# Gate sums inside the Fourier unit's products, constant products in TensorE's waits, and the cross-attention memory loaded early

## The reference

```python
g = (p[..., OFF_G:OFF_BR].astype(jnp.float32).reshape(b, l, N_GATE_KINDS, N_H).transpose(2, 0, 3, 1)
     + b_gates.astype(jnp.float32)[:, None, :, None])
...
h_f, s_f = mlstm_scan(q, k, v, g[0], jax.nn.log_sigmoid(g[1]), init[0])
...
u = p[..., OFF_F:OFF_QK].astype(jnp.float32).reshape(b, l, N_FG, FG)
fu = jnp.fft.fft2(u, axes=(1, 3), norm='ortho').real.astype(p.dtype).reshape(b, l, D_F)
...
y_m = (jax.nn.sigmoid(p[..., OFF_O:OFF_G]) * hm) @ w_mlstm
...
logf = jax.nn.log_sigmoid(f_logit.astype(jnp.float32) + fox_bf[l].astype(jnp.float32))
...
x = x + cross_attention(rmsnorm_2(x, norm_xa_g[l]), rmsnorm_2(mem, norm_mem_g[l]), ...)
...
g_logits = (hf @ wg).astype(jnp.float32) + bg.astype(jnp.float32)
e_logits = ((hf @ we).astype(jnp.float32) + be.astype(jnp.float32)).reshape(-1, N_GROUPS, EXPERTS_PER_GROUP)
```

## Time and profile before

| | |
|---|---|
| median of 3 runs | 1780.99 us (1780.74, 1780.99, 1786.05) |
| the profiled execution | 1787.18 us, span 1785.4 us |
| PE busy | 1686.0 us, 94% |
| DVE busy | 726.2 us, 41% |
| ACT busy | 400.8 us, 22% |
| mean granted TensorE clock | 0.977 of full speed |
| DMA | 374.35 MB, mean 210 GB/s over the span |

### The profile page before, as it was taken

The page is one execution under the profiler, slowest core; times in us unless marked ns, Lnnn a source line. Parts: engine busy times, 40 slices in busy tenths (PEclk is TensorE's granted clock), DMA queues, the critical chain, the costliest instruction groups (busy, mean ns, idle before and its releaser), DMA issues. The chain is left out here.

```text
span 1785.4 us, 21495 instructions
## 1 busy us (share of the span) xinstructions
PE 1686.0 (94%) x8607; PEld 951.5 (53%) x8607; DVE 726.2 (41%) x1337; ACT 400.8 (22%) x737; POOL 22.1 (1%) x29
## 2 busy tenths in 40 slices
PE   6998999998999999999999989999999999877987
PEld 3576456657886534443444333444478664454543
DVE  4644513656546011111111115974762424351425
ACT  5112112442214101010101031015641023210112
POOL 0000000000000000000000000000000000000001
PEclk9998999999999999999999999999999999988999
DMA  9421157101133999999999970411112231269974
GB/s 364 137 86 47 71 193 278 48 32 67 67 141 118 398 425 423 421 418 426 424 419 419 426 293 0 142 47 48 47 63 80 94 135 77 94 263 381 325 271 177
DMA packets 88934, 374.35 MB, mean 210 GB/s; under 512 B 9796, under 2 KB 10132, under 8 KB 73748
## 3 DMA queue, kind: packets, MB, share of 16 engines
q1 hardware_dynamic: 82084, 350.14, 50.0%
q10 hardware_dynamic: 3712, 12.06, 1.8%
q0 software_dynamic: 3056, 11.01, 1.7%
HBM read 466.51 MB, written 10.49 MB: 267 GB/s over the span
## 5 line engine op out<-in xcount | busy, mean ns | idle before, releaser
L2236 PE MATMUL bank<-H,weight_slots 128*128 128x512 f32 (+1 forms) x704 | 286.3, 565 | 4.1 <-ACT H L808 2.9
L2236 PEld LDWEIGHTS bank<-H,weight_slots 128*128 128x128 f32 x704 | 135.8, 195 | 149.2 <-issue 143.8
L2652 PE MATMUL bank<-weight_slots,SM 128*64 128x512 f32 x640 | 143.9, 595 | 9.4 <-DMA weight_slots<-in_w_up_e 9.4
L2337 PE MATMUL bank<-R,weight_slots 128*128 128x256 f32 x560 | 123.9, 380 | 0.0
L2680 PE MATMUL bank<-weight_slots,SM 128*64 128x512 f32 x384 | 114.6, 609 | 3.6 <-DMA weight_slots<-in_w_down_e 3.6
L2337 PEld LDWEIGHTS bank<-R,weight_slots 128*128 128x128 f32 x560 | 106.1, 190 | 15.7 <-issue 1.5
L2236 PE MATMUL bank<-R 128*128 128x128 f32 (+2 forms) x784 | 104.5, 286 | 9.5 <-DVE R L2088 6.2
L3028 PE MATMUL bank<-weight_slots,SM 128*32 128x256 f32 x1536 | 91.0, 390 | 21.3 <-DMA weight_slots<-in_expert_w_gate 11.5
L2236 PEld LDWEIGHTS bank<-R 128*128 128x128 f32 x784 | 94.4, 195 | 13.4 <-DVE R L2085 6.3
L2652 PEld LDWEIGHTS bank<-weight_slots,SM 128*64 128x64 f32 x640 | 45.4, 137 | 104.2 <-issue 84.1
L1762 DVE TENSOR_TENSOR R<-SM,bank 128x512 f32<-128x512 f32 x16 | 11.0, 687 | 217.7 <-PE bank L2652 217.7
(11 more groups left out here) (513 smaller groups left out, 2101.6 us busy)
## 6 DMA issues: line engine op xcount, KB each, us to landing
weight_slots<-in_expert_w_gate SPq DMA_DIRECT2D x51, 1024.0 KB
weight_slots<-in_expert_w_up SPq DMA_DIRECT2D x51, 1024.0 KB
R<-in_expert_w_down SPq DMA_DIRECT2D x51, 1024.0 KB
weight_slots<-in_w_up_e SPq DMA_DIRECT2D x24, 2048.0 KB, 17.3
weight_slots<-in_w_down_e SPq DMA_DIRECT2D x24, 2048.0 KB, 23.7
weight_slots<-in_w_in SPq DMA_DIRECT2D x18, 2048.0 KB, 9.5
weight_slots<-in_w_gate_e SPq DMA_DIRECT2D x16, 2048.0 KB, 17.0
weight_slots<-in_w_ada SPq DMA_DIRECT2D x12, 2048.0 KB, 10.7
```

What stands on the lines that cost most here:

```text
L2236: ins = nc.tensor.matmul(dst, lhsT, rhs, start=(i == 0), stop=(i == len(pairs) - 1))
L2337: ins = nc.tensor.matmul(bank_half(name, i, half)[:, TC * tile:TC * (tile + 1)], lhs[:, kk, m:m + 128], rhs[:, kk, :], start=(begins and k ...
L2652: ins = nc.tensor.matmul(b[64 * half:64 * half + 64, :], xs[:, 4 * rows + k, 64 * e:64 * e + 64], w[k][:, 512 * half:512 * half + 512], st ...
```

## The change

In unit `u`, the gate sums (now without bias products) stand behind P1 and the 12 transposes into rows behind P5; DVE and ACT do the gate arithmetic between the unit's additions and copies; all four folds stand behind the unit's last addition. The wait for the rows' copies before the q products is gone. The biases of gates, forget logits and router are broadcast to all partitions by the loads and added by DVE where it copied before. `keep_busy` multiplies constants (128 x 128 by 128 x 512) in four places: 2 before the k products, 3 before the last expert pair's down products, 6 before the ranking, 6 before `pick_rows`.

The memory is loaded by ACT in two DMAs behind unit `w_fourier`, into `H`'s context columns. It is transposed at its old place into banks 2, 3, 6 and 7, and copied by ACT. Its squares (ACT, behind the copy of P1) are summed with 32-column weights behind P5 of unit `w_mlstm`, and the four partial sums are folded behind P7; DVE scales the memory behind the unit's last addition. P1 of the unit waits only for heads 0 and 1, P2 for the rest.

```diff
+        m_rows = H[:, :, T:T + TC]
+        memT = R4[:, :].rearrange("p (k t) -> p k t", k=KD)
+        mem_sq = SM[:, 0:2048].rearrange("p (k t) -> p k t", k=KD)
+        MEM_BANKS = (2, 3, 6, 7)
...
-                sp.dma_start(rowb[0:1, 0:16], A["b_gates"].rearrange("a g h -> a (g h)")).then_inc(sem("rowb_in"), 16)
+                sp.dma_start(rowb[:, 0:16], A["b_gates"].rearrange("a g h -> a (g h)").broadcast_to([P, 16])).then_inc(sem("rowb_in"), 16)
...
+            u_copies("P1", "11")
             act.wait_ge(sem("gate_v"), 1)
             act.activation(absf, gts[:, :, :, 1, :], ACT.Abs).then_inc(sem("gate_s"), 1)
...
+            u_copies("P6", "12")
             act.wait_ge(*reached("rows_mm", 1))
-            act.activation(ig_r[:, 0:T], PS[1][0:36, :], ACT.Copy).then_inc(sem("rows_s"), 1)
+            act.activation(ig_r[:, 0:T], PS[2][0:36, :], ACT.Copy).then_inc(sem("rows_s"), 1)
+            u_copies("P7", "22")
+            u_copies("P4", "21")
...
             quarter_copies("w_fourier")
+            act.wait_ge(sem("thin_mm"), 1)
+            for t in range(2):
+                act.dma_start(m_rows[:, 4 * t:4 * t + 4, :], A["mem_2"][0, P * t:P * (t + 1), :].rearrange("p (q n) -> p q n", n=TC)).then_inc(sem("mem_in"), 16)
...
-            act.wait_ge(sem("S_mm"), 16)
-            act.dma_start(m_tok, A["mem_2"].rearrange("b (t p) d -> p (b t) d", p=P)).then_inc(sem("mem_in"), 16)
-            rms_squares(act, "nm", memT, sqc, TC, lambda k: act.wait_ge(sem("mT_ev"), k // 2 + 1))
-            rms_root(act, "nm", PS[5][:, 0:TC], std[:, T:T + TC])
-            quarter_copies("w_mlstm")
+            for j in range(4):
+                act.wait_ge(*reached("mT_mm", j + 1))
+                act.activation(memT[:, 2 * j:2 * j + 2, :], PS[MEM_BANKS[j]][:, :].rearrange("p (k t) -> p k t", k=2), ACT.Copy).then_inc(sem("mT_ev"), 1)
+            block_copies("w_mlstm", "P1", "11")
+            act.wait_ge(sem("attn_v"), 23 * NH)
+            for k in range(KD):
+                act.wait_ge(sem("mT_ev"), k // 2 + 1)
+                act.activation(mem_sq[:, k, :], memT[:, k, :], ACT.Square).then_inc(sem("rms_sq"), 1)
+            block_copies("w_mlstm", "P6", "12")
...
-            fold_u(2)
-            fold_u(3)
...
-            nc.vector.tensor_copy(gts, PS[0][:, 0:96].rearrange("p (t e c h) -> p t e c h", t=TA, e=2, c=2)).then_inc(sem("gate_v"), 1)
+            nc.vector.tensor_tensor(SM[:, 1024:1120].rearrange("p (t n) -> p t n", t=TA), PS[0][:, 0:96].rearrange("p (t n) -> p t n", t=TA),
+                                    rowb[:, 0:16].unsqueeze(1).broadcast_to([P, TA, 16]), ALU.add).then_inc(sem("gate_v"), 1)
...
+            for g in (2, 3, 0, 1):
+                fold_u(g)
+            dve.wait_ge(*reached("u_fold", 12))
             nc.vector.memset(cum_r, 0.0).then_inc(sem("rows_v"), 1)
...
-                rms_scale(dve, "nm", lambda k: memT[:, k, :], lambda k: H[:, k, T:T + TC], TC, std[:, T:T + TC], rstd2[:, T:T + TC], lambda k: v("mem", k))
...
-            plain_sums("w_mlstm", s2_mlstm, beside_mlstm, beside_last=lambda: weight_sums("brB0", s1, s2))
+            plain_sums("w_mlstm", s2_mlstm, beside_mlstm, beside_last=gate_weights)
+            rms_scale(dve, "nm", lambda k: memT[:, k, :], lambda k: H[:, k, T:T + TC], TC, std[:, T:T + TC], rstd2[:, T:T + TC], lambda k: v("mem", k))
...
+            def keep_busy(bank, times):
+
+                for i in range(times):
+                    nc.tensor.matmul(bank[:, :], ones, const[:, 0:512], start=True, stop=True)
...
-            wait_weights(pe, "k")
             for j in range(8):
                 b = take(j % 4, "conv_k", 3 * (j + 1) if j < 4 else 12 + 9 * (j - 3))
+                if j == 0:
+                    keep_busy(b, 2)
+                    wait_weights(pe, "k")
...
-                    first = [] if bias is None else [(ones[0:1, :], bias)]
-                    ins = product(dst[:, n * t:n * (t + 1)], first + [(parts[:, 128 * t:128 * (t + 1)], fold[:, 0:n])])
+                    ins = product(dst[:, n * t:n * (t + 1)], [(parts[:, 128 * t:128 * (t + 1)], fold[:, 0:n])])
...
-                   "P4": [(sem("quarter_ev"), ev + 5 + half) for half in range(2)], "P3": [(sem("quarter_add"), add + 2)] * 2})
-            thin_sum(take(0, "gate_v", 1), thin_gates, TA, 16, 2, rowb[0:1, 0:16]).then_inc(sem("gate_mm"), 1)
+                   "P4": [(sem("quarter_ev"), ev + 5 + half) for half in range(2)], "P3": [(sem("quarter_add"), add + 2)] * 2},
+                  behind={"P1": gates_summed, "P5": gates_turned})
...
-            pe.wait_ge(sem("rows_v"), 4)
             w = weights("q", KD)
...
-            rms_sum(pe, "nm", take(5, "rms_std", NORMS["nm"] + 1), sqc, TC)
-            pe.wait_ge(sem("attn_v"), 23 * 4)
-            seven_plain("w_mlstm", "mlstm", mlstm_in, mlstm_sums, s1_mlstm, s2_mlstm)
+            def memory_squares():
+                part = take(6, "rms_part", WIDE["nm"])
+                for k in range(KD):
+                    g = k % 4
+                    pe.wait_ge(sem("rms_sq"), KD * NORMS["nm"] + k + 1)
+                    nc.tensor.matmul(part[32 * g:32 * g + 32, 0:TC], ones[:, 0:32], mem_sq[:, k, :], start=(k < 4), stop=(k >= 4),
+                                     tile_position=(0, 32 * g)).then_inc(sem("rms_sum"), 1)
...
+            seven_plain("w_mlstm", "mlstm", mlstm_in, mlstm_sums, s1_mlstm, s2_mlstm, {"P1": (sem("attn_v"), 23 * 2), "P2": (sem("attn_v"), 23 * NH)},
+                        {"P5": memory_squares, "P7": memory_norm})
...
                 pe.wait_ge(sem("hidT_ev"), pair * 2 + 2)
+                if pair is last:
+                    keep_busy(PS[0], 3)
...
-            nc.tensor.matmul(b[:, 80:100], ones[0:1, :], rowb[0:1, 24:44], start=True, stop=True)
             thin_sum(b, thin, TT, 20, 5).then_inc(sem("rl_mm"), 1)
 
+            b = take(2, "token_slots", 2)
+            keep_busy(b, 6)
             pe.wait_ge(*reached("chosen", 1))
...
+            keep_busy(PS[0], 6)
             for name, value in (("xtok_v", 2 * TT), ("x_sq", 2 * TT), ("thin_ev", 5), ("g_v", 2), ("token_slots", 2)):
```

More of the change, by code:

```diff
@@ L64 @@
 KEY_BANKS = (0, 1, 4, 5)
-WIDE = {name: i + 1 for i, name in enumerate(["n1", "n2", "nf", "n3", "n4"])}
+WIDE = {name: i + 1 for i, name in enumerate(["n1", "nm", "n2", "nf", "n3", "n4"])}
 def key_done(j):
@@ L496, in build @@
         fourier_sums = [two(R6[:, 512 * i:512 * (i + 1)]) for i in range(4)]
-        mlstm_sums = [two(R4[:, 512 * i:512 * (i + 1)]) for i in range(4)]
+        mlstm_sums = [two(R2[:, 512 * i:512 * (i + 1)]) for i in range(4)]
         conv_sums = [two(c0_flat[:, 0:512]), two(c0_flat[:, 512:1024]), conv_in["12"], two(R2[:, 0:512])]
@@ L832, in _, with u_copies @@
             u_quarters = quarters(u_plain)
-            for which, quarter in (("P1", "11"), ("P6", "12"), ("P7", "22"), ("P4", "21")):
+            def u_copies(which, quarter):
                 for half in range(2):
@@ L908, in _ @@
                         gate_a(2 * h + 1)
-            act.wait_ge(sem("S_mm"), 16)
-            act.dma_start(m_tok, A["mem_2"].rearrange("b (t p) d -> p (b t) d", p=P)).then_inc(sem("mem_in"), 16)
-            rms_squares(act, "nm", memT, sqc, TC, lambda k: act.wait_ge(sem("mT_ev"), k // 2 + 1))
-            rms_root(act, "nm", PS[5][:, 0:TC], std[:, T:T + TC])
-            quarter_copies("w_mlstm")
+            for j in range(4):
[7 more added lines that the diff above has]
+            block_copies("w_mlstm", "P6", "12")
+            act.wait_ge(sem("rms_sum"), KD * NORMS["nm"] + KD)
+            act.activation(mem_parts, PS[6][:, 0:TC], ACT.Copy).then_inc(sem("rms_part"), 1)
+            block_copies("w_mlstm", "P7", "22")
+            act.wait_ge(sem("rms_fold"), WIDE["nm"])
+            act.activation(std[:, T:T + TC], PS[7][:, 0:TC], ACT.Sqrt, bias=small[:, 40:41], scale=1.0 / D).then_inc(sem("rms_std"), 1)
+            block_copies("w_mlstm", "P4", "21")
             def quarter_gates(name):
@@ L2342, in seven, with seven_plain @@
                         behind[which]()
-            def seven_plain(name, of, src, t, s1, s2):
+            def seven_plain(name, of, src, t, s1, s2, ready=None, behind=None):
                 ev, add = QUARTER_EV[name], QUARTER_ADD[name]
@@ L2348, in seven_plain @@
                       {"P6": [(sem("quarter_ev"), ev + 1 + half) for half in range(2)], "P7": [(sem("quarter_ev"), ev + 3 + half) for half in range(2)],
-                       "P4": [(sem("quarter_ev"), ev + 5 + half) for half in range(2)], "P3": [(sem("quarter_add"), add + 3 + half) for half in range(2)]})
+                       "P4": [(sem("quarter_ev"), ev + 5 + half) for half in range(2)], "P3": [(sem("quarter_add"), add + 3 + half) for half in range(2)]}, ready, behind)
             def seven_gates(name, of, src, t, s1, s2):
@@ L2392, in _, with gates_summed, gates_turned @@
             pe.wait_ge(sem("wsmall_in"), 80)
-            pe.wait_ge(sem("rowb_in"), 64)
```

(11 more changed lines are left out.)

92 lines of the change are left out of this document (43 added, 49 removed).

## The result

The changed kernel took 1756.79 us in the median of four runs (1755.57 to 1758.51), beside 1783.52 us for the kernel before in four runs. The ratio is 0.9839, with a 95% interval of 0.9814 to 0.9864: 28.7 us less, 24.3 to 33.2. (Every "less than before" in this document is worked out from such a ratio; the two medians themselves are 26.7 us apart.) The forecast was 27.9 us less than before, 1753 us, with a range of 1747 to 1763. The time is 3.8 us above 1753, and 2.5 us of that is the kernel before, whose median was 1780.99 us when the forecast was made. One of the eight runs of `gates_alone` in experiment 2, 2099.3 us at a granted clock of 0.80, was in a slow state and is left out of that kernel's ratio.

What follows compares the result with a forecast made beforehand. The prediction took PE's own chain, busy 94% of the span, to set the end. Its terms, 11.3 + 10.4 + 1.4 + 2.1 + 2.0 + 0.7 = 27.9 us, off the 1781.0 us median gave 1753 us, range 1747 to 1763.

Steps and rivals of the forecast that it cites:

- Fourier input, gates: From unit `u`'s end to the end of the q products, 42.4 us become 31.1: 11.3 us less.
- merge: Last head's end to P1 of `w_mlstm`, 14.4 us, with norm moved into the unit: 10.4 us less, bounds 8 to 11.
- before k: Constants in PE's 2.86 us wait before k bring the clock back sooner: 1.4 us less, bounds -0.6 to 1.9.
- forget logits: 8 of 16 small entries go, and perhaps the low-clock spell from 1163 us: 2.1 us less, bounds 1.3 to 3.0.
- last pair: Constants in the 3.64 us wait for a down weight warm the down products: 2.0 us less, bounds -1.3 to 2.6.
- router: Constants in the 6.43 us wait for `chosen` let ranking run warm: 0.7 us less, bounds -3.4 to 1.5.
- The reserve of DVE: Behind `u`, scans start at about 160.2 us; row chain ready about 170, wanted 183.4; kw products have 16 us in hand.
- the load stream keeps its time: Rival: first MoE's loads don't come earlier with PE, only 5 us remain, 1776 us; chance 0.04.
- Low clock in the units: Rival: inserted small products or transposes lower the clock inside the two units, 1.7 to 6.8 us, about 1757; chance 0.13.
- Late engines: Rival: DVE or ACT late in a unit brings the removed wait back, 4 to 10 us, about 1761; chance 0.08.
- Constants decide nothing: Rival: the clock follows other things and `keep_busy` gives nothing or outlasts its waits, 1757 to 1762 us; chance 0.05.
- Slower: Rival: inserts in `u` keep the clock at 1.2 GHz to the end of the q products, 1805 us; chance 0.02.

Runs made afterwards that it cites:

- gates_alone: Kernel before with only the Fourier input and gate part of the change, biases included: 1775.22 us, ratio 0.9948.
- experiment 2: The change's three parts (gates, memory, constants) each put alone into the kernel before, and the whole: 1775.22, 1773.77, 1780.24 and 1756.36 us.
- experiments 1: Kernel before profiled again without any edit: 1783.64 us beside 1784.83 us, ratio 0.9995.
- memory_alone: Kernel before with only the memory part (early load, transposes behind the last head, norm inside unit `w_mlstm`): 1773.77 us, ratio 0.9939.
- experiment 5: Changed kernel with four 128 x 128 transposes in place of each product of constants: 1759.70 us, ratio 0.9861.
- experiment 3: Changed kernel with 14 or 28 memsets delaying DVE's row chain behind unit `u`: 1759.28 us (ratio 0.9857) and 1772.32 us (ratio 0.9930).
- experiment 4: Changed kernel with the memory's two loads issued at the old place, behind the last head's S products: 1765.37 us, ratio 0.9884.
- constants_alone: Kernel before with only the products of constants before k, the last pair's down products and around the ranking: 1780.24 us, ratio 0.9978.
- dve_later_12: Changed kernel with 14 memsets, 12.8 us, ahead of DVE's row chain behind unit `u`: 1759.28 us, ratio 0.9857.
- memory_late: The kernel of experiment 4: changed kernel with the memory's two loads issued at their old place: 1765.37 us, ratio 0.9884.

## Why the forecast was right, step by step

The mechanism was right in every part. Of the sizes, the largest was 1.8 us too big and the small ones some 2.2 us too small in all, so that the sum came out within 1 us is luck in part.

| term | forecast | less, by stretches | what it is |
|---|---|---|---|
| Fourier input, gates | 11.3 | 9.5 (12.2 in the first pair of profiles) | experiments 1, 2 |
| merge | 10.4 | 10.2 to 10.6 | `memory_alone` 10.2 to 10.6 |
| before k | 1.4 | 1.3 to 1.5 | lost with half the fill in experiment 5 |
| forget logits | 2.1 | 1.85 + 1.57 = 3.4 | past its bound of 3.0 |
| last pair | 2.0 | 2.6 | the upper bound |
| router | 0.7 | 1.0 | in five of eight traces; 0.4 us are lost in three |
| sum | 27.9 | 28.0 to 28.6 | measured 28.7 and 27.1 |

The sum leaves out the stretches that no edit touches. The two profiled executions themselves are 31.6 us apart in span, with draws of the clock, of the experts and of the time behind PE's last product in it, so the agreement of the sum with 28.7 us is no finer than those.

**The Fourier term.** The step that failed is "from the unit's end to the end of the q products the kernel now takes 42.4 us". 2.7 us of that was low clock in one execution; three other traces with the same code there have 27.70 us for the q products, though one of them lost 1.07 us just ahead of them. It was offset in part by the small entries: the forecast put 0.16 us on each of the 12 that stay, and they took 1.26 / 12 = 0.105 us; the transposes took 0.11 us each. 42.4 - 2.7 - 30.2 = 9.5. The profiles show 12.2 us only because the first one of before carried that spell. The covers held: no wait on PE between the thin product and the q products, and DVE's and ACT's gate steps ended at 137.7 us for transposes at 142.5 us.

**The reserve of DVE.** Right to 1.0 us in the scans' start, and experiment 3 shows 13.0 us where the prediction had 170 against 183.4, 13.4 us. The 16 us for the kw products were not reached by a test, since the rows bind first.

**The merge.** P1 came 2.2 us behind the head's last product (forecast 2.4), and squares and fold took 1.4 us in the unit (forecast 1.6). The first addition of `brB0`, said to be covered with 1.4 us left, shows just that:

```profile
420.41 3.26 DVE L786 SCALAR_TENSOR_TENSOR H<-R,vec,SM 128x256 f32<-128x256 f32 x8
425.09 0.69 DVE L1518 TENSOR_TENSOR R<-R,bank 128x512 f32<-128x512 f32 x1 [1.43 <-PE bank L2369]
```

What the prediction had not seen is what experiment 4 found: the new layout alone would have made the load slower, so the early issue was worth 7.7 us there, not the 2.4 us of the old wait. The prediction could cost the load at nothing only because it is early.

**The small ones.** Before k, 0.2 us of the gain were paid ahead of the k products: from the start of the old wait, or of the fill, to the first of them it is 3.07 us in after and was 2.86. The forget logits' eight remaining entries cost 0.10 us, not 0.16, and the low spell behind them went whole. Of the four traces with the 16 old entries three have that spell and `constants_alone` has not, while none of the nine others has it, so its 1.6 us are not wholly the edit's. The last pair gave the full 2.6 us, in every trace with the constants. The router did not: the ranking and the first products of `pick_rows` ran warm each time, but in `constants_alone`, `dve_later_12` and `memory_late` the second 32 products of `pick_rows` then took 5.44 us instead of 3.82, and the stretch was 19.7 us against 19.3 before. The prediction had left such a fall out.

**The loads of the first MoE** kept their distance to PE: 593.66 us before and 593.35 after, waits for `w_up` 9.4 us in ten waits in both traces. The rival "the load stream keeps its time" is out.

**The rivals.** Low clock in the units: none, in any of the nine traces with the gates inside `u`. Late engines: none, in the changed kernel PE has no new wait for DVE or ACT up to `brB0`. Constants decide nothing: out by `constants_alone` and by 16.55 against 13.95 us. Slower: out.

## What to carry to other kernels

Before a stall is priced from one profile, look at whether its low-clock share is there in a second execution: here 2.7 us of an 11.3 us term were not the kernel's, and errors of like size on the other side hid it. Small dependent work put between dense products costs only its own entries (0.11 us each) as long as the engine that feeds it has a unit's length of cover, and the cover can be measured by delaying that engine. A fill of constants pays up to the length of the wait and costs its full length beyond it, and paid nothing here where loads set the pace.

## What the runs showed of the hardware

The same code draws a spell of low clock in one execution and none in another. The stretch of the four heads is 204.1, 205.8 or 207.4 us in the 12 traces in which PE did not wait ahead of it, with zero, one or two spells of low clock, some 3.4 us long, each costing some 1.65 us. Two products with the same shape differ by their neighbours: 16-column entries took 0.16 us when one-row products stood between them and 0.105 us when not. The clock rises under float32 transposes alone, with PE doing nothing else since it stood empty (at 408.7 us in before, near 398.8 us in `memory_late`). Each 512 KB half of the memory, in 1 KB pieces, took 10.7 us (the median of the two) when issued together with a 2 MB weight load, and 4.2 to 5.0 us when issued 3.4 us ahead of one; the whole 1 MB in one load of larger pieces took 8.5 us beside a weight load.
